# Expert weights in 2 MB stretches: one transfer fills two neighbouring places of the weight ring

## The chip, the cores and the metric

The kernel runs on one core of one Trainium2 chip, as one program with one launch. The metric is the device time in microseconds (us); lower is better. Before the change it is 2817.83 us, the median of three runs (2816.88 to 2820.12).

TensorE (PE in the profile) multiplies, VectorE (DVE) and ScalarE (ACT) do the elementwise work, SyncE (SP) issues nearly all transfers, and 16 DMA engines move the data.

## The reference

One sequence of 256 tokens of width 1024 goes through three transformer blocks in fp32: a block with three attention branches and a mixture of experts, a block with neighbourhood attention and pooling, and a block with a short convolution. The change touches only the mixture of experts:

```
logits = xt @ router_w + router_b;  top_v, top_e = top_k(logits, 4);  gate = softmax(top_v)
for each of 32 experts e, with the rows of the tokens that chose e:
    hb = xb @ w1[e] + b1[e]            # w1[e]: 1024 x 2048
    g, u = hb[:, :1024], hb[:, 1024:]
    g = min(g, 7);  u = clip(u, -7, 7)
    y = ((u + 1) * g * sigmoid(1.702 * g)) @ w2[e] + b2[e]    # w2[e]: 1024 x 1024
out[token] += gate * y
```

The weights of one expert are 12 MB in fp32, those of all 32 experts 384 MB. They are read from HBM once (and 12 MB more for the over turn named below).

## The kernel before

**The ring.** All weights pass through `ring`, a tile of 128 partitions with places of 8 KB each. In the expert stage eight places are in use. A slot is one use of a place: 1 MB, that is two chunks of 128 rows by 1024 columns. Slot j of the stage lies in place j % 8.

**A turn.** The stage is a loop of 16 turns, each for two experts, and after it an "over turn" of 12 slots for the busiest expert's tokens beyond 64. A turn uses 24 slots in this order: 0 to 3 gate columns of expert 0, 4 to 7 its up columns, 8 to 11 gate of expert 1, 12 to 15 up of expert 1, 16 to 19 down of expert 0, 20 to 23 down of expert 1 (`MOE_SLOTS`).

**What a slot goes through.** SP waits until the slot eight before has been used, then issues the transfer (`load_pair`, L692), which adds 16 to the semaphore of the place when it has landed. ACT waits for that semaphore and for the slot four before to have been used, and rounds the weights to `w_high` (`high`, L929; `w_high` has four places). DVE subtracts, in place over the ring, and leaves the rest as `w_low` (`low`, L2353). PE multiplies with `w_high` and then with `w_low` (`rows_gemm`, L1635, 4 + 4 matmuls per slot). The last matmul of a slot releases its place: it adds to `slots_used`, or, for every fourth slot, to `psum_full`. This is `MOE_RELEASE`, and SP waits for it.

**The order on the engines** is written out by hand. ACT: slots 4, 5, 6; copy of the gate rows (L964); slots 7, 8, 9, 10; copy of the up rows (L964); a small copy (L969); slot 11; the swish (L975); slots 12, 13, 14; L964; slots 15, 16, 17; rounding of the hidden layer of expert 0 (L982); slot 18; and so on to slot 3 of the next turn. DVE: slots 4 to 10; the gate half of expert 0 (L2380, L2386); slots 11 to 15; the up half of expert 0 (L2380, L2390, L2393); slot 16; the low part of the hidden layer (L2396); slots 17, 18; and later, near the turn's end, the sum of the results (L2405). PE cannot begin slot 16, the first of the down product, before L2396 has ended.

**The layout in HBM.** `slots(w)` lays a slot's 1 MB out in one stretch, with 8 KB for each partition, so that the slots of one half of one expert follow one another.

The functions that the change touches:

Of the kernel before, what the change touches and what calls it, by code (L numbers as in the profile page):

```python
# [16 lines left out]
P = 128  # L17
D = 1024
T = 256
DC = D // P  # L20
# [3 lines left out]
N_EXPERTS, TOP_K = 32, 4  # L24
# [20 lines left out]
SLOT = 2 * D  # L45
# [3 lines left out]
RING2, HIGHS = 8, 4  # L49
# [87 lines left out]
class Plan:  # L137
# [15 lines left out]
    def placed(self):  # L153

        while len(self.place) < len(self.stream):
            s = len(self.place)
            self.next = (self.next + 1) % self.places if s else 0
            self.place.append(self.next)
            self.before.append(self.holder.get(self.next))
            self.times[self.next] = self.times.get(self.next, 0) + 1  # L160
            self.landing.append(self.times[self.next])
            self.holder[self.next] = s

# [186 lines left out]
PLAN = make_plan()  # L350
# [56 lines left out]
def build(nc, ins, out):  # L407
    with ExitStack() as ctx:
        def sb(name, shape, dt=F32):
            return ctx.enter_context(nc.sbuf_tensor(name, shape, dt))  # L410
# [3 lines left out]
        def sem(name):  # L414
            if name not in sems:
                sems[name] = ctx.enter_context(nc.semaphore(name))
            return sems[name]
# [7 lines left out]
        ring = sb("ring", [P, RING, SLOT])  # L425
# [62 lines left out]
        at = 4096  # L488
# [56 lines left out]
        landed = [sem(f"slot_landed{i}") for i in range(RING)]  # L545
# [25 lines left out]
        def await_slot(pe, s):  # L571

            pe.wait_ge(landed[PLAN.place[s]], 16 * PLAN.landing[s])
# [6 lines left out]
        def slot_ap(s, rows=2, cols=D):  # L580
            return ring[:, PLAN.place[s], 0:rows * cols].rearrange("p (k n) -> p k n", k=rows)
# [33 lines left out]
        class Turn:  # L615
# [40 lines left out]

            def await_slot(self, eng, j):

                place = PLAN.place[PLAN.moe_slot + j]
                times = j // RING2 + 1 if self.x else PLAN.landing[PLAN.moe_slot + j]  # L660
                eng.wait_ge((landed_x if self.x else landed)[place],
                            self.turn * (16 * TURN_SLOTS // RING2) + 16 * times)
# [18 lines left out]

        def load_pair(sp, c, before_turn=None, slots=range(TURN_SLOTS)):

            for j, at in enumerate(slots):
                name, e, k, half = MOE_SLOTS[at]
                if j < RING2 and before_turn:
                    before_turn(j)
                else:
                    c.await_used(sp, j - RING2)
                src = ins[name][c.experts[e]][half * (DC // 2) + k // 2].rearrange("p (k n) -> p k n", k=2)  # L690
                place = PLAN.place[PLAN.moe_slot + j]
                sp.dma_start(slot_ap(PLAN.moe_slot + j), src).then_inc((landed_x if c.x else landed)[place], 16)  # L692

        def rounds_loop(eng, before_pairs, body):

# [9 lines left out]
        landed_x = [sem(f"slot_landed_x{i}") for i in range(RING2)]  # L705
# [13 lines left out]
        def _(sp):  # L719
# [15 lines left out]
            def before_first(j):  # L735
                if PLAN.before[PLAN.moe_slot + j] is not None:
                    await_release(sp, PLAN.before[PLAN.moe_slot + j])

            load_pair(sp, first_turn(0), before_first)
            with sp.Fori(1, PAIRS) as i:  # L740
                load_pair(sp, first_turn(i))
            load_pair(sp, over_turn(busiest_expert(sp)), None, OVER_AT)
            with sp.If(many(sp) > CAP):

# [23 lines left out]
        def _(act):  # L768
# [104 lines left out]
            def high_piece(n):  # L873

                s = PLAN.slots[f"mpiece{n}"]
                if n < 2:
                    await_release(act, PLAN.piece_before[n])
                else:
                    await_unit(act, U[f"mpiece{n - 2}"])
                await_slot(act, s)  # L880
                act.activation(piece_parts(n)[0], slot_ap(s, DC, 2 * P), ACT.Copy).then_inc(sem("piece_high_ready"), 1)
# [179 lines left out]
            def high_parts(until):  # L1061

                while highs[0] < len(PLAN.split_at) and PLAN.split_at[highs[0]] < until:
                    m = highs[0]
                    s = PLAN.split_at[m]
                    cols = PLAN.stream[s][5]
                    if m < HIGHS:
                        await_release(act, moe_end - HIGHS + m)
                    else:
                        await_release(act, PLAN.split_at[m - HIGHS])  # L1070
                    await_slot(act, s)
                    act.activation(high_ap(m, cols), slot_ap(s, 2, cols), ACT.Copy).then_inc(sem("w_high_ready"), 1)  # L1072
                    highs[0] += 1
# [128 lines left out]
        def _(pe):  # L1202
            def gemm(name, k_chunks, n_chunks, operands, parts_ready=None, halves_last=False):
# [17 lines left out]
                def await_parts(k):  # L1221
                    if k % 2 == 0:
                        if parts_ready:
                            parts_ready(k)
                        await_slot(pe, slots[k // 2])
# [1532 lines left out]
```

## Time and profile before

| | |
|---|---|
| device time, median of 3 runs | 2817.83 us (2816.88 to 2820.12) |
| span of the profiled execution | 2811.8 us |
| own time of the profiled execution | not listed apart; the median of the runs is 6.0 us above its span |
| PE busy | 2709.9 us, 96% |
| DVE busy | 2100.9 us, 75% |
| ACT busy | 1575.8 us, 56% |
| mean granted TensorE clock | 0.975 |
| expert transfers | 396 of 1024 KB |
| one turn of the expert stage (from issue to issue of slot 4) | 64.73 us |

The expert stage lies between about 440 and 1500 us of the span, slices 7 to 21 of the 40 in which the page cuts the span. Busy shares over the whole span hide that this stage has limits of its own: here DVE and the DMA engines are busy nearly all the time as well, so the stage has to be read by itself. In a row, "A <- B" after a time means that A sat idle until B released it. A row with x3 or x4 merges neighbouring instructions of one kind: its start is that of the first, its length that of all.

### The profile page before, as it was taken

What the parts mean: (1) busy time and instruction counts of PE and PEld (TensorE: products, weight loads), DVE (VectorE), ACT (ScalarE), POOL (GpSimd) and SP (SyncE); (2) the same over time, 40 slices, a digit from 0 to 9 for tenths busy, and PEclk for the clock granted to TensorE, in tenths of its full rate; (3) what the DMA queues carried; (4) which work ended last, traced back from release to release, by engine and by line L of the source; (5) the groups of instructions that cost most, each with busy time, mean ns of one, the idle gap of its engine ahead of it and who ended that gap; (6) DMA issues with size and microseconds to landing.
All of it is one profiled execution on the core that took longest, in us unless ns stands there. A gap on an engine that the chain in (4) does not pass through costs nothing.

```text
span 2811.8 us, 43791 instructions
## 1 busy us (share of the span) xinstructions
PE 2709.9 (96%) x17682; PEld 2472.9 (88%) x17682; DVE 2100.9 (75%) x1766; ACT 1575.8 (56%) x1410; POOL 0.4 (0%) x6
## 2 busy tenths in 40 slices
PE   6999999999999999999998999999989999999998
PEld 5889888888888888888886999999879999999998
DVE  6347649999999999999998787785545866754553
ACT  0045318888888888888884443353434434432442
POOL 0000000000000000000000000000000000000000
PEclk9999898999999999999998999999999999999999
DMA  9744448999999999999995876776317767754561
GB/s 391 255 164 135 151 171 329 381 380 388 389 385 392 390 390 393 394 390 382 386 379 199 297 251 255 258 266 243 142 65 251 283 222 262 270 178 165 165 194 62
DMA packets 172691, 776.11 MB, mean 276 GB/s; under 512 B 12272, under 2 KB 38000, under 8 KB 121616
## 3 DMA queue, kind: packets, MB, share of 16 engines
q1 hardware_dynamic: 168640, 768.71, 72.3%
q10 hardware_dynamic: 3920, 5.49, 0.7%
q8 instruction: 103, 1.69, 0.2%
q14 instruction: 28, 0.23, 0.0%
HBM read 773.10 MB, written 1.05 MB: 275 GB/s over the span
## 4 chain that ended last, share of the span: by engine, by line
PE 82%; DVE 11%; issue 3%; ACT 3%; DMA 0%; SPq 0%; DVEq 0%; ACTq 0%
PE psum L1257 38%; PE psum L1635 18%; PE psum L1211 7%; DVE w_low L2353 6%; PE psum L1675 4%; PE psum L1612 2%; PE psum L1653 2%; PE psum L1336 2%; ACT w_high L929 1%; PE psum L1355 1%; PE psum L1397 1%; PE psum L1492 1%; DVE arena L2380 1%; PE psum L1445 1%; PE psum L1520 1%
## 5 line engine op out<-in xcount | busy, mean ns | idle before, releaser
L2353 DVE TENSOR_TENSOR w_low<-ring,w_high 128x2048 fp32r<-128x2048 f32 x396 | 885.1, 2287 | 31.6 <-ACT w_high L929 20.5
L929 ACT ACTIVATE w_high<-ring 128x2048 fp32r<-128x2048 f32 x396 | 736.2, 1905 | 47.9 <-PE psum L1635 47.9
L1072 ACT ACTIVATE w_high<-ring 128x2048 fp32r<-128x2048 f32 (+1 forms) x199 | 362.4, 1829 | 561.2 <-PE psum L1257 478.0
L2489 DVE TENSOR_TENSOR w_low<-ring,w_high 128x2048 fp32r<-128x2048 f32 (+1 forms) x199 | 432.7, 2184 | 320.3 <-ACT w_high L1072 317.4
L1257 PE MATMUL psum<-h_high,w_high 128*128 128x256 f32 x2080 | 588.5, 283 | 21.6 <-ACT h_high L1085 20.4
L1257 PE MATMUL psum<-h_high,w_low 128*128 128x256 f32 x2080 | 590.6, 284 | 0.0
L1257 PE MATMUL psum<-h_low,w_high 128*128 128x256 f32 x2080 | 588.2, 284 | 0.0
L1257 PEld LDWEIGHTS psum<-h_high,w_high 128*128 128x128 f32 x2080 | 399.6, 192 | 24.1 <-issue 22.2
L1257 PEld LDWEIGHTS psum<-h_low,w_high 128*128 128x128 f32 x2080 | 394.9, 191 | 0.0
L1257 PEld LDWEIGHTS psum<-h_high,w_low 128*128 128x128 f32 x2080 | 394.5, 190 | 0.0
L1635 PE MATMUL psum<-w_high,xg 128*128 128x512 f32 x1056 | 296.0, 402 | 0.6 <-ACT xg L957 0.6
L1635 PE MATMUL psum<-w_low,xg 128*128 128x512 f32 x1056 | 291.7, 398 | 0.1
L1924 DVE SCALAR_TENSOR_TENSOR mod_sums<-ring,cs,mod_sums 128x1024 f32<-128x1024 f32 x203 | 257.4, 1282 | 12.7 <-DMA ring<-in_mod_w 8.5
L1257 PE MATMUL psum<-m_high,w_high 128*128 128x256 f32 x880 | 247.7, 281 | 0.8 <-DVE arena L2529 0.8
L1257 PE MATMUL psum<-m_low,w_high 128*128 128x256 f32 x880 | 247.2, 281 | 0.0
L1257 PE MATMUL psum<-m_high,w_low 128*128 128x256 f32 x880 | 247.2, 281 | 0.0
L1635 PEld LDWEIGHTS psum<-w_low,xg 128*128 128x128 f32 x1056 | 197.3, 188 | 54.6 <-DVE w_low L2353 7.0
L1635 PEld LDWEIGHTS psum<-w_high,xg 128*128 128x128 f32 x1056 | 196.7, 189 | 45.5 <-issue 0.8
L1635 PE MATMUL psum<-w_high,hid 128*128 128x512 f32 x528 | 153.8, 414 | 22.9 <-DVE hid L2396 22.9
L1257 PEld LDWEIGHTS psum<-m_high,w_high 128*128 128x128 f32 x880 | 165.8, 188 | 1.0 <-DVE arena L2529 0.9
L1257 PEld LDWEIGHTS psum<-m_low,w_high 128*128 128x128 f32 x880 | 165.8, 188 | 0.1
L1257 PEld LDWEIGHTS psum<-m_high,w_low 128*128 128x128 f32 x880 | 165.8, 188 | 0.0
(288 smaller groups left out, 3441.5 us busy)
## 6 DMA issues: line engine op xcount, KB each, us to landing
ring<-in_exp_w SPq DMA_DIRECT2D x396, 1024.0 KB, 8.7
ring<-in_ffn_w SPq DMA_DIRECT2D x135, 1024.0 KB, 5.3
ring<-in_mod_w SPq DMA_DIRECT2D x96, 1024.0 KB, 5.6
ring<-in_ffn_w SPq DMA_DIRECT2D x40, 768.0 KB, 4.7
ring<-in_w_in SPq DMA_DIRECT2D x24, 1024.0 KB, 8.9
ring<-in_even_w_in SPq DMA_DIRECT2D x12, 1024.0 KB, 7.2
ring<-in_conv_w_in SPq DMA_DIRECT2D x12, 1024.0 KB, 5.1
ring<-in_w_branch SPq DMA_DIRECT2D x6, 1024.0 KB, 5.5
```

The lines of the kernel that those rows point to most:

```text
L929: act.activation(high_ap(j, D), slot_ap(PLAN.moe_slot + j), ACT.Copy).then_inc(sem("expert_high_ready" + c.x), 1)
L1072: act.activation(high_ap(m, cols), slot_ap(s, 2, cols), ACT.Copy).then_inc(sem("w_high_ready"), 1)
L1211: mm = pe.matmul(unit(u0 + j // 4)[:, (j % 4) * T:(j % 4 + 1) * T], w[:, k % 2, (c0 + j) * P:(c0 + j + 1) * P], rhs(k), start=(k == 0 and ...
L1257: return pe.matmul(unit(u0 + j // 4)[:, (j % 4) * T:(j % 4 + 1) * T], w[:, k % 2, j * P:(j + 1) * P], h[:, k, :], start=first, stop=stop, ...
L1336: mm = pe.matmul(unit(u)[:, at:at + 1], mod_sums[:, MOD_BUFFERS[n][c], j * P:(j + 1) * P], ones[:, 0:1], start=True, stop=True)
L1612: mm = pe.matmul(cols[:, n, :, part * CAP:(part + 1) * CAP], h_nat[:, b, k * P:(k + 1) * P], sel[:, b, :, :], start=(b == 0), stop=(b == T ...
L1635: mm = pe.matmul(u[:, cols], x_parts(k), w[:, k % 2, cols], start=(k == 0 and w is wh), stop=(k == DC - 1 and w is wl), skip_group_check=True)
L1653: mm = pe.matmul(u[:, k * CAP:(k + 1) * CAP], moe_buf(rows)[:, k * P:(k + 1) * P], const("fold"), start=True, stop=True)
L1675: mm = pe.matmul(c.unit(name)[:, (k % 4) * T:(k % 4 + 1) * T], moe_buf(f"y_rows{e}")[:, k * P:(k + 1) * P], moe_buf(f"selT{e}"), start=(e ...
L1924: last = dve.scalar_tensor_tensor(part, w[:, k % 2, :], cond, part, ALU.mult, ALU.add)
L2353: dve.tensor_tensor(low_ap(PLAN.moe_slot + j, D), slot_ap(PLAN.moe_slot + j), high_ap(j, D).bitcast(F32), ALU.subtract).then_inc(sem("expe ...
L2489: dve.tensor_tensor(low_ap(s, cols), slot_ap(s, 2, cols), high_ap(m, cols).bitcast(F32), ALU.subtract).then_inc(sem("w_split"), 1)
```

## The change

The layout keeps four chunks (two slots) together, so that a partition's 16 KB for slots j and j+1, with j even, lie in one piece. `load_pair` goes through the slots in steps of two: it waits for the release of the odd slot's place, and issues one transfer of 2 MB into places j % 8 and j % 8 + 1. Only the even place's semaphore is incremented, and whoever waits for an odd slot waits for the semaphore of the even one. The bookkeeping of how often a place has been filled (`placed`) leaves the odd places of this stage out. The layouts of the other stages, their transfers, and the order of work on ACT, DVE and PE stay.

```
@@ placed @@
-            self.times[self.next] = self.times.get(self.next, 0) + 1
+            with_other = self.stream[s] is None and self.next % 2
+            self.times[self.next] = self.times.get(self.next, 0) + (0 if with_other else 1)
@@ await_slot @@
+                j -= j % 2
                 place = PLAN.place[PLAN.moe_slot + j]
@@ load_pair @@
-            for j, at in enumerate(slots):
+            for j, at in list(enumerate(slots))[::2]:
                 name, e, k, half = MOE_SLOTS[at]
                 if j < RING2 and before_turn:
                     before_turn(j)
+                    before_turn(j + 1)
                 else:
-                    c.await_used(sp, j - RING2)
-                src = ins[name][c.experts[e]][half * (DC // 2) + k // 2].rearrange("p (k n) -> p k n", k=2)
+                    c.await_used(sp, j + 1 - RING2)
+                src = ins[name][c.experts[e]][half * (DC // 4) + k // 4]
                 place = PLAN.place[PLAN.moe_slot + j]
-                sp.dma_start(slot_ap(PLAN.moe_slot + j), src).then_inc((landed_x if c.x else landed)[place], 16)
+                two = ring[:, place:place + 2, :].rearrange("p s n -> p (s n)")
+                sp.dma_start(two, src).then_inc((landed_x if c.x else landed)[place], 16)
@@ slots @@
-        pairs = w.reshape(N_EXPERTS, DC // 2, 2, P, -1, D)
-        return pairs.transpose(0, 4, 1, 3, 2, 5).reshape(N_EXPERTS, -1, P, SLOT)
+        fours = w.reshape(N_EXPERTS, DC // 4, 4, P, -1, D)
+        return fours.transpose(0, 4, 1, 3, 2, 5).reshape(N_EXPERTS, -1, P, 2 * SLOT)
```

SP's order at the start of the loop over turns, slots 0 to 3 of a turn, before:

```order
L692 ISA [waits slots_used]
L692 DMA ring<-in_exp_w 128x2048
L655 REGISTER_ALU
L692 ISA [waits slots_used]
L692 DMA ring<-in_exp_w 128x2048
L655 REGISTER_ALU
L692 ISA [waits slots_used]
L692 DMA ring<-in_exp_w 128x2048
L653 ISA
L692 ISA [waits psum_full]
L692 DMA ring<-in_exp_w 128x2048
```

The same place after the change:

```order
L696 ISA [waits slots_used]
L696 DMA ring<-in_exp_w 128x4096
L654 ISA
L696 ISA [waits psum_full]
L696 DMA ring<-in_exp_w 128x4096
```

Two transfers of twice the width stand where four stood, and each waits for what the odd slot's transfer waited for.

ACT's order from slot 8 to slot 12 of a turn, before (`slot_landed0` is the semaphore of place 0; L964 and L969 copy out of PSUM, L975 is the swish):

```order
L929 ACTIVATE w_high<-ring 128x2048 [waits slot_landed0]
L655 REGISTER_ALU
L929 ACTIVATE w_high<-ring 128x2048 [waits slot_landed1,slots_used]
L655 REGISTER_ALU
L929 ACTIVATE w_high<-ring 128x2048 [waits slot_landed2,slots_used]
L638 REGISTER_ALU
L964 ACTIVATE arena<-psum 128x1024 [waits psum_full]
L638 REGISTER_ALU
L969 ACTIVATE arena<-psum 128x256 [waits psum_full]
L661 REGISTER_ALU [waits psum_full]
L929 ACTIVATE w_high<-ring 128x2048 [waits slot_landed3]
```

and after:

```order
L933 ACTIVATE w_high<-ring 128x2048 [waits slot_landed0]
L656 REGISTER_ALU
L933 ACTIVATE w_high<-ring 128x2048 [waits slot_landed0,slots_used]
L656 REGISTER_ALU
L933 ACTIVATE w_high<-ring 128x2048 [waits slot_landed2,slots_used]
L639 REGISTER_ALU
L968 ACTIVATE arena<-psum 128x1024 [waits psum_full]
L639 REGISTER_ALU
L973 ACTIVATE arena<-psum 128x256 [waits psum_full]
L933 ACTIVATE w_high<-ring 128x2048 [waits slot_landed2,psum_full]
```

The order of the work is the same; slots 8 and 9 now wait for one semaphore, and so do slots 10 and 11. A register instruction has gone ahead of slot 11 (one more stands ahead of slot 12 instead, outside these rows).

## Rows read from the trace of the kernel before

**Rows 1.** The page: busy time, then DMA share and GB/s in 40 slices.

```profile
PE 2709.9 (96%) x17682; PEld 2472.9 (88%) x17682; DVE 2100.9 (75%) x1766; ACT 1575.8 (56%) x1410; POOL 0.4 (0%) x6
...
DMA  9744448999999999999995876776317767754561
GB/s 391 255 164 135 151 171 329 381 380 388 389 385 392 390 390 393 394 390 382 386 379 199 297 251 255 258 266 243 142 65 251 283 222 262 270 178 165 165 194 62
```

**Rows 2.** Busy time in one turn: us; PE, PEld, DVE, ACT, POOL; clock, DMA, GB/s.

```profile
942.90:1007.63 64.73, 63.27 (x326) 53.08 (x325) 62.79 (x41) 56.95 (x45) 0.00 (x0) 1.00 0.96 388
```

**Rows 3.** Waits, 500 to 1480 us: total us, times, longest.

```profile
ACT w_high L929 <- PE psum L1635: 45.0, 35, 2.4
...
PE psum L1635 <- DVE hid L2396: 22.0, 15, 1.5
DVE w_low L2353 <- ACT w_high L929: 16.2, 30, 1.5
```

**Rows 4.** Waits of SP's queue, 500 to 1480 us.

```profile
SPq L692 <- PE psum L1635: 769.1, 363, 6.6
```

**Rows 5.** Chain of waits, 960 to 992 us: start, length, what.

```profile
971.37 2.29 DVE w_low L2353
973.66 0.61 DVE arena L2380
...
974.83 0.02 ACTq L661
974.85 0.06 issue
974.91 0.04 ACTq L655
...
975.29 1.91 ACT w_high L929
...
983.84 2.29 DVE w_low L2353
...
990.12 0.61 DVE hid L2396
990.73 0.12 issue
990.85 1.20 PE psum L1635 x4
```

**Rows 6.** Timeline of SP: issues of slots 4, 5, 8, 9, 10, 11.

```profile
942.90 0.33 SPq L692 DMA_DIRECT2D ring<-in_exp_w  x1
944.77 0.33 SPq L692 DMA_DIRECT2D ring<-in_exp_w  x1
...
955.61 0.33 SPq L692 DMA_DIRECT2D ring<-in_exp_w  x1
957.47 0.33 SPq L692 DMA_DIRECT2D ring<-in_exp_w  x1
959.33 0.33 SPq L692 DMA_DIRECT2D ring<-in_exp_w  x1
961.20 0.33 SPq L692 DMA_DIRECT2D ring<-in_exp_w  x1
```

**Rows 7.** The tile ring: issue to landing of slots 4, 8, 9, 10, 11, in order.

```profile
DMA to landing us min/median/max: 4.7/4.7/4.7
...
DMA to landing us min/median/max: 4.8/4.8/4.8
...
DMA to landing us min/median/max: 6.1/6.1/6.1
...
DMA to landing us min/median/max: 7.2/7.2/7.2
...
DMA to landing us min/median/max: 7.8/7.8/7.8
```

**Rows 8.** DMA with a full queue, 8 KB rows (970 to 990 us).

```profile
DMA packets 1165, 8.49 MB, mean 424 GB/s; under 512 B 129, under 2 KB 129, under 8 KB 129
```

**Rows 9.** DMA with a full queue, 4 KB rows (1738 to 1742 us, FFN weights).

```profile
DMA packets 440, 1.68 MB, mean 419 GB/s; under 512 B 31, under 2 KB 31, under 8 KB 440
```

**Rows 10.** Timeline of ACT: slots 4 to 6, 7 to 10, 12 to 14, 15 to 17.

```profile
955.56 5.57 ACT L929 ACTIVATE w_high<-ring 128x2048 fp32r<-128x2048 f32 x3 [1.11 <-PE psum L1635]
...
961.99 7.31 ACT L929 ACTIVATE w_high<-ring 128x2048 fp32r<-128x2048 f32 x4
...
975.29 5.51 ACT L929 ACTIVATE w_high<-ring 128x2048 fp32r<-128x2048 f32 x3
...
981.60 5.52 ACT L929 ACTIVATE w_high<-ring 128x2048 fp32r<-128x2048 f32 x3
```

**Rows 11.** DVE's slots by form, in the expert stage and in the later blocks.

```profile
L2353 DVE TENSOR_TENSOR w_low<-ring,w_high 128x2048 fp32r<-128x2048 f32 x362 | 809.1, 2287 | 27.1 <-ACT w_high L929 16.2 <-DVE arena L2405 7.1
...
L2489 DVE TENSOR_TENSOR w_low<-ring,w_high 128x2048 fp32r<-128x2048 f32 x137 | 312.0, 2291 | 197.3 <-ACT w_high L1072 195.3 <-DVE mod_sums L1924 0.8
```

## The prediction, made before the changed kernel was run

> **What bounds the kernel now.** I read the page first. PE is busy 96% of the span, and in slices 7 to 20, the expert stage, the DMA engines read 9 in every slice at 380 to 394 GB/s, where later stages read 5 to 7 [rows 1]. That looks like a stage bound by its transfers, which larger transfers could help. So the second view is the list of waits of the stage. It holds no wait of ACT, DVE or PE for a landing at all: ACT waits for PE, PE for DVE, DVE for ACT [rows 3]. SP in turn waited 769.1 us of these 980 us for PE to release places [rows 4]. So the transfers go as fast as PE frees places, and no engine is held up by one. The third view is one turn by itself: 64.73 us, of which PE is busy 63.27, DVE 62.79, ACT 56.95, and the DMA share is 0.96 [rows 2]. Four resources are within 12% of one another, so what counts is their order. The chain of waits, the fourth view, gives it: in the first half of the turn it runs along DVE (slot 10 at 971.37, the gate half, slots 12 to 15 with slot 15 at 983.84, the low part of the hidden layer at 990.12) and enters PE at 990.85 [rows 5]. PE sits idle just before that, 22.0 us in 15 turns, 1.47 each [rows 3]. Whatever holds DVE up between slot 10 and slot 16 therefore lengthens the turn one for one. What holds PE up there costs nothing until the 1.47 us are used.
>
> The question is then by how much the landings lead their users, since the change makes each even slot land with its odd neighbour. The lead is smallest after the two places in a turn where SP waits longest (up to 6.6 us [rows 4]) and the queue runs dry: ahead of slot 4 and ahead of slot 8. I follow slot 8.
>
> **What the change does to the landings.** Before, in the turn of rows 2: slot 8 is issued at 955.61 and lands 4.8 later, at 960.4; slot 9 at 957.47, landing at 963.6; slot 10 at 959.33, landing at 966.5; slot 11 at 961.20, landing at 969.0 [rows 6, 7]. With a full queue the rate is 424 GB/s [rows 8], so 1 MB (1.049e6 bytes) takes 2.47 us, a pair 4.95. The landings of slots 8 to 11 lie 3.2, 2.9 and 2.5 apart. So after a dry queue two transfers lose 0.7 and 0.4 us against the full rate, 1.1 to 1.2 together, and the fourth, issued 5.6 us after the restart, loses nothing.
>
> After, the pair 8/9 is issued when slot 9 was, 957.47. A first transfer of 1 MB on a dry queue needs 4.8; the second MB adds 2.47: it lands at 964.7. Pair 10/11 is issued at 961.20, while the first still runs, and lands 4.95 + x later, at 969.7 + x. Here x is what the second transfer after a dry queue loses. Its bounds are 0 (as in the full queue) and 1.2 (all that three transfers lost before). I take 0.45, the row of the third transfer, since it was issued 3.72 after the first one, and the second pair is issued 3.73 after its first. Pairs 12/13 and 14/15 follow at 4.95 each: 974.6 + x and 979.6 + x.
>
> **What ACT and DVE do with that.** ACT runs slots 7 to 10 from 961.99 in steps of 1.80 (7.31 for four, 1.9 for one [rows 10]), so slot 8 starts at 963.8 and slot 10 at 967.4. Slot 8 is now 0.9 late and slot 9 with it. Slot 10 waits for 969.7 + x, which is 2.3 + x late, and ends at 971.6 + x. DVE started slot 10 at 971.37 [rows 5]: the cover was 2.1 us, and it is used up. DVE is late by 0.25 + x. After slot 10 ACT still has L964, L969 and slot 11 before DVE's own gate half is done; with the rows' spacing of 3.0 us, slot 11 is rounded by 974.6 + x, when DVE wants it. The swish and slots 12 and 13 only follow DVE. Slot 14 would start at 978.9 (two steps after 975.29), now at 979.15 + x, but lands at 979.6 + x. It pushes L964 and slot 15, which came 2.7 after slot 14 (981.60 [rows 10]), to 982.3 + x, ending at 984.2 + x. DVE took slot 15 at 983.84 [rows 5]: it is now late by 0.4 + x in all, not in addition. From slot 16 on ACT has more lead on DVE than the lateness (slot 18 about 0.6, slot 20 about 0.2, and each then has over 2 us to DVE), so nothing more comes on top.
>
> Per turn: 0.4 + 0.45 = 0.85 us. Lower end: x = 0, and rows of 16 KB move a little faster; from 4 KB to 8 KB rows the rate went from 419 to 424 GB/s [rows 8, 9], 1.2%, so up to 0.06 a pair, 0.2 over four pairs: 0.2 per turn. Upper end: 0.4 + 1.2 = 1.6 per turn. I give the wider rows nothing in the sum.
>
> **The rest of the edits.** Slots 4 to 7: the pair 4/5 starts on a dry queue too. Issued at 944.77, where slot 4 was issued at 942.90 and took 4.7 [rows 6, 7], it lands at 944.77 + 4.7 + 2.47 = 951.9, and pair 6/7 at 956.9 + x. ACT takes slots 4 to 6 from 955.56 in steps of 1.8, so slot 6 at 959.2 [rows 10]: leads of 3.6 and 1.8, covered. Slots 16 to 23 and 0 to 3 are moved at most 2.5 + 0.7 + x, and the DMA queue again runs dry ahead of slot 4, so lateness is not handed from turn to turn. SP has half as many issues (12 a turn); it only ever waits, so nothing comes of it. The extra register instruction ahead of slot 12 on ACT stands on the chain: one such step with its issue took about 0.1 [rows 5]. It falls in the 0.15 by which slot 14's landing is the later of the two limits, so it adds nothing unless x is small. Layout in HBM and semaphore bookkeeping cost no time. Everything outside the stage keeps its transfers.
>
> **The sum.** 15 turns x 0.85 = 12.8; the first turn's slot 10 has about 0.1 more lead, 0.75; the over turn has slots 8 to 11 but no 12 to 15, so 0.25 + 0.45 = 0.7. Together 14.2 us on a span of 2811.8. The median of the runs lies 6.0 above the span, and nothing of the change touches that: 2817.8 + 14.2 = 2832. Lower end 16.5 x 0.2 = 3, upper end 16.5 x 1.6 = 26: 2821 to 2844.
>
> **A rule and the trace.** Before the change the landings with a full queue come at 2.47 us per MB, all data, so a transfer's fixed part costs nothing there; on a dry queue it shows as 4.8 - 2.47 = 2.3 us, and a turn has two dry starts before and after. The Trainium skill, "DMA: Bandwidth & Descriptors", section "Anatomy of one DMA", gives a fixed cost of about 2 us for each transfer besides bytes over 436 GB/s, and "SBUF — State Buffer" advises the largest single transfer where the transfers bind. Taken per transfer in sequence, that rule would save 12 x 2 = 24 us a turn, which the landings 2.5 us apart speak against. Taken per dry start it agrees with the 2.3 of the trace, and by it the first pair would land at 957.47 + 2 + 4.8 = 964.3 instead of 964.7.
>
> **The rivals.** (a) The cover holds: the pair lands about 0.3 us sooner than I add up (a first transfer of 2 MB may hide its slow start better, x = 0, faster wide rows), so slot 10 comes within 0.1 of DVE's time. Then 0.0 to 0.3 per turn, up to 5 us: 2818 to 2823, say 2820. For it: the cover of 2.1 against a lateness of 2.3 is a near thing. Against it: x was not 0 at either of the two places in rows 7.
> (b) The restart costs its full 1.2 us with two transfers as it did with three, or more, because each is twice as long: 1.6 and up per turn, 2844 and more. PE's 1.47 us of idle don't help, as they come from the same wait. For it: the loss may go with bytes after a dry start, not with the time from issue. Against it: the fourth transfer, 5.6 us on, lost nothing.
> (c) Faster. The mechanism: DVE and ACT read and write the ring while the DMA engines fill it, and fewer, wider rows disturb them less; the place is DVE's 24 slots a turn at 2287 ns. It decides if DVE's slot gets shorter by more than the 0.2 to 0.85 us a turn that the landings cost. But DVE takes 2287 in this stage at a DMA share of 0.96 and 2291 in the later blocks at 5 to 7 tenths [rows 11, 1]: there is nothing to give back. A gain of 0.5%, 11 ns a slot, 0.27 a turn would be 4 us: 2814 with no lateness at all.
> (d) The change doesn't do what it says: the rows of 16 KB are cut in two for the DMA engines. Then only the wide rows' 0.2 goes, and the sum above stands, as it doesn't use them.
>
> **How the numbers follow.** The forecast with (d), 0.35 to 1.4 us a turn or 2824 to 2840: 62%. (a): 20%. (b): 13%. (c): 5%. A measurement of this kernel tells about 0.2%, 5.6 us, from no change; the borders are 2812.2 and 2823.5. (a) lies within, (b) and the forecast above, and of (c) half would be within: slower 0.75, same 0.22, faster 0.03. The predicted time is that of the forecast, 2832. The range leaves out the far parts of (b) and of (c): 2818 to 2845.
>
> **What would show it.** In the profile after: 198 expert transfers of 2048 KB; a new wait "ACT w_high <- DMA ring" in every turn, some 2.5 us at slot 10 and under 1 us at slots 8 and 14; DVE's wait for ACT up from 16.2 us by 10 to 15; PE's wait for the hidden layer up from 1.47 to about 2.3 a turn; the turn at 65.6 instead of 64.73; DVE's slot unchanged at 2287 ns. If the ACT waits are there and the turn is not longer, the cover held, and (a) is right. If no ACT wait for a landing shows, the step on the pair's landing is wrong. If the turn is longer but PE's wait for the hidden layer is not, the loss lies in the second half of the turn, and my chain is wrong.

## The result

The changed kernel takes 2842.11 us (median of 4 runs, 2839.3 to 2843.05) against 2817.36 us, a ratio of 1.0093 with a 95% interval of 1.0076 to 1.0109. It is 0.9% slower, 24.7 us. A second series on another occasion gave 2840.4 against 2814.02, 1.0072 (1.0048 to 1.0097). The ratios and their intervals are the recorded ones, here and below. They are not the quotient of the two medians, and the two can lie 0.2% apart. The forecast was slower, at 2832, in a range of 2818 to 2845.

The page of the profile after: busy times, DMA share, and the costliest groups that answer to the expert stage.

```profile
PE 2722.8 (96%) x17682; PEld 2483.2 (87%) x17682; DVE 2105.5 (74%) x1766; ACT 1585.0 (56%) x1410; POOL 0.4 (0%) x6
...
DMA  9744448999999999999995776777417767754451
...
L2357 DVE TENSOR_TENSOR w_low<-ring,w_high 128x2048 fp32r<-128x2048 f32 x396 | 889.1, 2287 | 44.5 <-ACT w_high L933 32.9
L933 ACT ACTIVATE w_high<-ring 128x2048 fp32r<-128x2048 f32 x396 | 744.6, 1909 | 108.7 <-DMA ring<-in_exp_w 56.9
...
ring<-in_exp_w SPq DMA_DIRECT2D x198, 2048.0 KB, 9.9
```

The busy times moved by less than 1%, and DVE's slot takes the same 2287 ns as in [rows 11]. What is new is a releaser: ACT now waits for the DMA of `ring`. The list of waits, 500 to 1480 us, against [rows 3]:

```profile
ACT w_high L933 <- DMA ring<-in_exp_w: 50.2, 75, 1.5
...
DVE w_low L2357 <- ACT w_high L933: 27.6, 52, 1.5
PEld psum L1639 <- issue: 24.4, 14, 1.8
...
PE psum L1639 <- DVE hid L2400: 16.6, 11, 1.5
...
PE psum L1639 <- DVE w_low L2357: 11.4, 15, 0.9
...
PE psum L1639 <- ACT w_high L933: 6.0, 4, 1.5
```

There are 75 waits of ACT for a landing in 15 turns, five a turn. DVE's wait for ACT went from 16.2 to 27.6, and PE has a second stop, for DVE's `w_low`, of 0.76 a turn. The stop of 1.5 us ahead of slot 16 is still there in every turn: 11 times the view puts it down to DVE, and 4 times to ACT (6.0 us), 22.6 us together against 22.0 before.

Now the turns one by one, from DVE's slot 4 to its next: length, busy us of PE, PEld, DVE, ACT, POOL, then granted clock, DMA share, GB/s. The first row of each block is all 16 turns together, the others are single turns. Of before:

```profile
436.57:1476.47 1039.90, 1016.91 (x5195) 853.12 (x5194) 1004.75 (x641) 911.68 (x704) 0.00 (x0) 1.00 0.96 388
...
762.58:828.72 66.14, 64.67 (x326) 54.13 (x325) 62.95 (x41) 57.23 (x45) 0.00 (x0) 0.97 0.94 381
```

Of after:

```profile
434.62:1493.82 1059.20, 1022.54 (x5191) 856.11 (x5190) 1008.98 (x641) 920.98 (x704) 0.00 (x0) 0.99 0.93 380
...
899.41:966.58 67.17, 64.78 (x326) 54.17 (x325) 63.16 (x40) 57.67 (x45) 0.00 (x0) 0.97 0.92 375
966.58:1031.92 65.34, 63.23 (x326) 53.03 (x325) 62.96 (x40) 57.51 (x45) 0.00 (x0) 1.00 0.94 385
```

All 16 turns together took 1059.2 us instead of 1039.9, 19.3 more. Two things are in it. A turn at full clock takes 65.3 to 65.7 instead of 64.73 (the first and the last turn have other lengths in both kernels). And turns with a granted clock of 0.97 take 66.96 to 67.17 where a full one takes 65.3 to 65.7, some 1.6 more. Before had two of these among its 16 turns; after had five, and a sixth fall of the clock in its first turn.

Outside the stage the two spans differ by 8.4 us (27.7 less 19.3), though nothing there was changed but the over turn, for which the sum had 0.7 us. From the end of these windows to the end of the span it is 2811.8 - 1476.5 = 1335.3 before and 1345.7 after:

```profile
1476.47:2811.80 1335.33, 1291.97 (x10213) 1261.34 (x10211) 849.21 (x763) 533.31 (x448) 0.15 (x2) 0.98 0.61 212
...
1493.82:2839.50 1345.68, 1301.89 (x10213) 1270.86 (x10211) 849.64 (x763) 533.26 (x448) 0.15 (x2) 0.97 0.60 211
```

The same 10213 matmuls kept PE busy 9.9 us longer, at a lower granted clock. Added up from the trace, the clock stood at the lower of its two levels for 54 us of this stretch before and for 83 after. Less half of that time, the stretch is 1308 and 1304 us, and in all fourteen profiles between 1304 and 1310. In the twelve profiles of the experiments, none of which changes more of that part than its over turn, the stretch lies between 1336.3 and 1345.6, with 59 to 76 us at the lower level. So the profiled execution of before was the quickest of them all there, and that of after the slowest. About 19 of the 25 us lie in the expert stage. The rest goes with the clock behind it, where the profiles differ even between kernels that are alike there. Whether the changed stage has a part in it is not shown.

### The profile page after: what moved, and what is told of

Read it like the earlier page. It is cut to its first block and busy times, and to the rows that moved or that the text cites. A ratio compares the mean times of both kernels' runs of the same rounds, so it can differ in the third digit from the quotient of the medians.

```text
span 2839.5 us, 43045 instructions
## 1 busy us (share of the span) xinstructions
PE 2722.8 (96%) x17682; PEld 2483.2 (87%) x17682; DVE 2105.5 (74%) x1766; ACT 1585.0 (56%) x1410; POOL 0.4 (0%) x6
## 5 line engine op out<-in xcount | busy, mean ns | idle before, releaser
L2357 DVE TENSOR_TENSOR w_low<-ring,w_high 128x2048 fp32r<-128x2048 f32 x396 | 889.1, 2287 | 44.5 <-ACT w_high L933 32.9
L933 ACT ACTIVATE w_high<-ring 128x2048 fp32r<-128x2048 f32 x396 | 744.6, 1909 | 108.7 <-DMA ring<-in_exp_w 56.9
```

Of the source, the lines that this page charges most:

```text
L933: act.activation(high_ap(j, D), slot_ap(PLAN.moe_slot + j), ACT.Copy).then_inc(sem("expert_high_ready" + c.x), 1)
L2357: dve.tensor_tensor(low_ap(PLAN.moe_slot + j, D), slot_ap(PLAN.moe_slot + j), high_ap(j, D).bitcast(F32), ALU.subtract).then_inc(sem("expe ...
```

## The experiments

In all that follow, "a turn" is read as above, from DVE's slot 4 to the next, at full clock where nothing else is said. The times stand against runs of the kernel before on the same chip.

**1. The late issue alone.** SP waits as in the changed kernel, transfers stay as before:

```
                 if j < RING2 and before_turn:
-                    before_turn(j)
-                else:
-                    c.await_used(sp, j - RING2)
+                    if j % 2 == 0:
+                        before_turn(j)
+                        before_turn(j + 1)
+                elif j % 2 == 0:
+                    c.await_used(sp, j + 1 - RING2)
```

> The old layout and 1 MB transfers with a semaphore each, but SP waits for the odd slot's place before it issues both of a pair, one right behind the other. Theory A (the loss needs the late issue and the joint signal together: only then does slot 10 come later than the 2.1 us by which ScalarE leads VectorE there): slot 8 lands about 4.8 after the issue, 1.5 before ScalarE wants it, slot 10 at most 0.5 late, inside the cover; turn 64.7 to 64.9 us, time within 3 us of before. Rival B (the late issue alone is the loss, by an idle DMA queue): turn 65.4, time +20 us or more. Rival C (the layout in HBM or the wide rows are the loss): as before, turn 64.73.

2818.45 against 2816.27, ratio 0.9999 (0.9989 to 1.0009). The turn is 64.7:

```profile
958.61:1023.31 64.70, 63.23 (x326) 53.06 (x325) 62.74 (x40) 56.96 (x45) 0.00 (x0) 1.00 0.94 389
```

Waiting for the odd place costs nothing. Rival B falls. The issues and landings of slots 8 to 11 in this turn, each issue followed by its own landing:

```profile
957.94 0.33 SPq L694 DMA_DIRECT2D ring<-in_exp_w  x1
...
DMA to landing us min/median/max: 4.7/4.7/4.7
...
958.46 0.33 SPq L694 DMA_DIRECT2D ring<-in_exp_w  x1
...
DMA to landing us min/median/max: 6.8/6.8/6.8
...
961.66 0.33 SPq L694 DMA_DIRECT2D ring<-in_exp_w  x1
...
DMA to landing us min/median/max: 6.0/6.0/6.0
...
962.17 0.33 SPq L694 DMA_DIRECT2D ring<-in_exp_w  x1
...
DMA to landing us min/median/max: 8.0/8.0/8.0
```

Counted from the first issue they land at 4.7, 7.3, 9.7 and 12.2, some 2.5 apart: issued in twos, 0.52 apart, the transfers of 1 MB lose nothing after the dry start. In [rows 6] they were issued 1.9 apart and lost 1.1 to 1.2.

**2. The joint signal alone.** Whoever uses an even slot waits for both landings:

```
+                for q in (j, j + 1) if j % 2 == 0 else (j,):
+                    place = PLAN.place[PLAN.moe_slot + q]
                     ...
+                    eng.wait_ge((landed_x if self.x else landed)[place],
                     ...
```

> The old layout, 1 MB transfers issued as before, but whoever needs an even slot waits until the odd one has landed too. Theory A: slot 10 is rounded 1.6 to 1.7 us later, inside the 2.1 us of cover; turn 64.73 to 64.9, time within 3 us of before, and ScalarE shows waits for landings at slots 10 and 14. Rival B: as before. A rival D (the joint signal alone is the loss) would give a turn of 65.4 and +20 us.

2821.6 against 2816.27, 1.0012 (0.9996 to 1.0028); eleven turns at full clock take between 64.69 and 64.95 and one 65.21.

```profile
1159.75:1224.44 64.69, 63.23 (x326) 53.06 (x325) 62.75 (x40) 57.24 (x45) 0.00 (x0) 1.00 0.97 389
```

ACT's busy time went up by 0.3 us a turn here, the usual turn did not. Rival D, with its 20 us, falls too: the median is 5 us higher, and the interval ends at 0.28%, 8 us.

**3. The layout alone.** New layout, and transfers of 1 MB, 8 KB rows that lie 16 KB apart:

```
+                src = ins[name][c.experts[e]][half * (DC // 4) + k // 4][:, k // 2 % 2 * SLOT:(k // 2 % 2 + 1) * SLOT] \
                     ...
```

> The new layout, but transfers of 1 MB as before: rows of 8 KB, 16 KB apart in HBM. Theory A: nothing changes, turn 64.73, landings 2.48 us apart, time within 2 us of before. Rival C: the landings are further apart than 2.5 us and the turn is longer.

2814.97 against 2816.27, 0.9993 (0.9977 to 1.001), with turns of 64.71. Rival C falls as far as the layout goes: where the rows lie in HBM has no part in it. Rows of 16 KB come only with transfers of 2 MB, so this run does not test them.

**What 1 to 3 leave open.** Theory A says that the late issue and the joint signal together are the loss. No run has just these two, with transfers of 1 MB. Experiment 1 allows an estimate. There slots 9 and 11 land 6.61 and 11.58 us after DVE's slot 4, in the median of the turns. The pairs of the changed kernel, whose first issue comes at the same time (0.67 before slot 4 in both), land at 7.05 and 11.94. So the joined transfer itself comes 0.4 later than two single ones issued one right behind the other. With the joint signal on the landings of experiment 1, slot 8 would be 0.9 to 1.1 late for ACT, inside DVE's cover of 1.27, and DVE would be 0.3 to 0.5 late at slot 10, where the changed kernel has 0.79. By this estimate the late issue and the joint signal explain about half of DVE's lateness, and the later landing of the joined transfer the other half.

**4 and 5. Which pairs.** The changed kernel with pairs for some slots and single transfers for the others (`JOINT` lists the pairs; single odd slots have their own semaphore again):

```
+                both = j - j % 2 in JOINT
+                if both and j % 2:
+                    continue
                 ...
+                    c.await_used(sp, j + both - RING2)
```

Once with all pairs but 8/9 and 10/11:

> As after, but slots 8 to 11 of each turn come in four transfers of 1 MB, each with its own issue and signal; the other twenty slots in ten pairs. Theory A: the loss is that of slots 8 to 11, and slots 12 to 15 have just enough lead: turn 64.7 to 64.9, time within 4 us of before. Rival E (every pair costs a little): turn about 65.3, +16 us or more.

2818.86 against 2816.27, 1.001 (0.9996 to 1.0024). Six turns take 64.7 and seven 64.9 to 65.3. The rest is at slot 15, where DVE is 0.23 late in the median turn. One more turn had a fall of the clock (67.7). The first turn took 67.5 instead of 65.6, which I did not follow up. Once with these two pairs only:

> As before, but slots 8/9 and 10/11 come as pairs of 2 MB with one signal, the other twenty slots in single transfers. Theory A: nearly the whole loss of after: turn 65.3 (0.6 at slot 10; slots 12 to 15 land one by one again), 12 to 20 us over before. Rival E (every pair costs a little): 2 to 4 us over before.

2834.1 against 2814.02, 1.0054 (1.0033 to 1.0075), 20 us. Turns of 65.3 to 65.6, and four more with a clock of 0.97. Of 12 pairs in a turn, two carry most of the loss: 20 us where the changed kernel, in the same series, has 26 (experiment 8), and nearly all of the longer turn.

**6 and 7. Each of the two by itself**, one run each.

> As before, but slots 8/9 come as one pair; slots 10 and 11 and all others single. Theory A: the pair lands at 7.7 after its issue and slot 10, 2.45 to 2.5 later, about 1.0 past ScalarE's time, within the 2.1 us of cover: turns without a fall of the clock 64.73. A rival H (any late landing there costs its own lateness): about 65.0 to 65.3.

2818.72 against 2816.38, with turns of 64.8 to 65.0 and no fall of the clock. DVE's seven slots 4 to 10, first in the kernel before:

```profile
958.15 15.51 DVE L2353 TENSOR_TENSOR w_low<-ring,w_high 128x2048 fp32r<-128x2048 f32 x7 [0.41 <-DVE arena L2405]
```

and with this pair:

```profile
890.36 15.67 DVE L2373 TENSOR_TENSOR w_low<-ring,w_high 128x2048 fp32r<-128x2048 f32 x7 [0.41 <-DVE arena L2425]
```

That is 0.16 longer. The lateness is not at slot 10, which is covered as expected, but at slot 8: ACT's lead there was 1.26 to 1.27, and slot 8 was 1.3 to 1.4 late. I had not worked out that cover. The turns lie between theory A's 64.73 and rival H's 65.0 to 65.3.

> As before, but slots 10/11 come as one pair, all others single. Theory A: the pair lands about when slot 11 did, 1.6 past ScalarE's time for slot 10 or a little more, within the cover: 64.73. Rival H: 65.0 or more.

2826.09 against 2816.38, 9.7 us in a single run. Nine of the 16 turns are as before, and two more within 0.2 us. Two are at 65.4, two of those with a low clock read 67.2 and 67.8 instead of 66.1, and the last 66.8 instead of 65.2. The cover is just used up: after ACT's slot 10 DVE starts its own 0.1 later in the median turn, where it had 2.08. Without the falls of the clock (none with pair 8/9, four with pair 10/11, two before), the 16 turns are longer by 0.15 and 0.35 us each on the mean, and by 0.8 with both pairs (experiment 5). Rival H, that a late landing costs its whole lateness, does not hold: slot 8 came 1.3 to 1.4 late and cost 0.16.

**8. The changed kernel again.**

> The changed kernel once more, beside the kernel before on the same chip. Theory A with the clock: turns without a fall of the granted clock about 65.3 to 65.6 us, five to seven turns with one at about 67, time 18 to 26 us over before. If the extra 8 us in the stages after the experts belonged to the change, they would be there again; if they are the run's own clock, the time outside the expert stage is within 5 us of the other profiles.

2840.4 against 2814.02, 26 us. The 16 turns took 1060.7 us, with six falls of the clock; the rest of the span 2841.4 - 1497.9 = 1343.5. Stage and falls are those of the first profile.

**9. VectorE late without any change to the transfers.** One instruction more in the kernel before, whose result nobody uses:

```
                 low(c, 4, 5, 6, 7, 8, 9, 10)
+                dve.tensor_reduce(small[:, 461:462], vecs[:, 0:560], AX_X, ALU.max)
                 gate_half(0)
```

> The kernel before, its transfers untouched, with one more VectorE instruction of about 0.6 us a turn (a maximum over 560 columns, its result unused) between slot 10 and the gate half of expert 0. Theory A: a lateness of VectorE there lengthens the turn one for one, 64.73 to about 65.35, as in after; and if TensorE's longer idle time is what makes the granted clock fall in more turns, five to seven turns instead of two or three read about 66.9: 16 to 20 us over before. Rival F (the falls come with the transfers or by chance): 10 us over before and two or three such turns. Rival G (the loss in after is not VectorE's slot 10): no longer turn, the instruction is hidden.

2830.53 against 2814.02, 1.0053 (1.0036 to 1.0069), 16.5 us. Two turns of its profile:

```profile
828.42:895.32 66.90, 64.79 (x326) 54.23 (x325) 63.57 (x42) 57.21 (x45) 0.00 (x0) 0.97 0.93 376
895.32:960.68 65.36, 63.26 (x326) 53.07 (x325) 63.39 (x42) 56.93 (x45) 0.00 (x0) 1.00 0.95 385
```

The turn is 0.63 longer, for an instruction of 0.73 that delays DVE's next one by 0.65. And there are four turns at a clock of 0.97, where five to seven were expected and before had two. PE's stops, 500 to 1480 us, are nearly those of after, and no engine waits for a landing:

```profile
PE psum L1635 <- DVE hid L2396: 21.9, 15, 1.5
PE psum L1635 <- DVE w_low L2353: 9.7, 15, 0.7
```

This is nearly the picture of the changed kernel, made with DVE alone. Rival G falls. Of rival F the transfers fall as the cause of the longer turn; chance does not yet, since experiments 1 to 3 have three falls each without a longer turn, and four is only one more.

**10. Twice that**, over 1120 columns (1.32 us).

> As the kernel with the late VectorE, but the unused maximum is over 1120 columns, about 1.3 us. Theory A: turns of 64.73 + 1.3 less the 0.08 that the first left hidden, about 65.95, still one for one, and as many or more turns with a lower clock at 1.55 us each: 24 to 34 us over before. Rival: TensorE's longer idle time makes the clock fall in nearly every turn: 40 us and more.

2843.94 against 2816.38, 1.01 (1.0083 to 1.0117), 27.6 us. Turns of 65.93, and nine at 67.4 to 67.9:

```profile
968.42:1035.89 67.47, 64.78 (x326) 54.23 (x325) 64.17 (x41) 57.22 (x45) 0.00 (x0) 0.97 0.93 373
1035.89:1101.82 65.93, 63.25 (x326) 53.08 (x325) 64.00 (x42) 56.97 (x45) 0.00 (x0) 1.00 0.94 383
```

Again nearly one for one (1.20 for an instruction of 1.32, whose start overlaps its neighbour's end), and 1.54 for each fall of the clock, within theory A's 24 to 34 us. Nine falls speak against chance. With PE's idle time of 1.5, 2.1 and 2.7 us a turn, 2, 4 and 9 of the 16 turns had a lower clock.

**11. A shorter chain, in the kernel before.** DVE does the up half of expert 0 ahead of slot 15, PE turns the gate rows of expert 1 ahead of slot 15, and DVE's slot 16 comes behind the hidden layer:

```
-                low(c, 11, 12, 13, 14, 15)
-                up_half(0, 16)
-                low(c, 17, 18)
+                low(c, 11, 12, 13, 14)
+                up_half(0, 15)
+                low(c, 16, 17, 18)
@@ PE
-                project("up1", 1, 12)
-                turn_rows("gate1_turn", "gate1", "gate_rows", 1)
+                project("up1", 1, 12, lambda: turn_rows("gate1_turn", "gate1", "gate_rows", 1))
```

The function given to `project` runs ahead of its last slot, 15. The edits of `project` and of the order of the PSUM units are left out here.

> The kernel before with the chain that the experiments point to made shorter: VectorE does the up half of expert 0 ahead of slot 15 instead of behind it, and slot 16 behind the hidden layer's low part; TensorE turns the gate rows of expert 1 ahead of slot 15. Theory A (VectorE from slot 10 to the hidden layer bounds half the turn, and TensorE has 1.47 us idle there): about 1 us less a turn, 63.7, and fewer turns with a lower clock: 12 to 20 us under before. If the second half of the turn or the transfers bound it as closely: less than 5 us.

2811.59 against 2814.02, 0.9983 (0.9969 to 0.9998): 2.4 us faster than the kernel before. The expected 1 us a turn, 12 to 20 us in all, is not there:

```profile
886.94:951.48 64.54, 63.71 (x326) 52.98 (x325) 62.75 (x41) 56.82 (x45) 0.00 (x0) 1.00 0.97 390
```

The turn is 0.19 shorter. DVE is at slot 18 at the same time after its slot 4 as before, 34.89: the order changed, its sum of work did not, and it has no gap to give. But PE's 1.45 us in one piece is gone (its longest stop is 0.7), and in this profile the clock did not fall once in 16 turns: 1033.9 us for the stage. Over whole runs this does not show: the granted clock is 0.974 in the median of the 12 runs, and 0.975 in the 22 of before.

**12. The changed kernel with that chain.**

> The changed kernel with the shorter chain of the kernel with the up half sooner. Theory A: slot 10 is as late as in after, so the turn is 64.53 + 0.6, about 65.15; if the falls of the clock hang on the 1.5 us of idle ahead of the hidden layer, which is gone here, there are none or few in the stage: 6 to 12 us over before. If they hang on the whole idle time of a turn, two to six remain and it is 10 to 20 us over before.

2835.66 against 2816.38, 1.0066 (1.0044 to 1.0087). That is 19 us over before, where 6 to 12 were expected. The turn is 65.5 to 65.9, not 65.15, and the clock did not fall in the 16 turns; all four runs have a granted clock of 0.975 to 0.977, those of the changed kernel in the first series 0.969 to 0.971. One of its turns on DVE:

```profile
834.37 13.50 DVE L2361 TENSOR_TENSOR w_low<-ring,w_high 128x2048 fp32r<-128x2048 f32 x6 [0.41 <-DVE arena L2413]
848.33 2.29 DVE L2361 TENSOR_TENSOR w_low<-ring,w_high 128x2048 fp32r<-128x2048 f32 x1 [0.46 <-ACT w_high L933]
...
865.27 0.69 DVE L2404 TENSOR_TENSOR hid<-arena,hid 128x512 fp32r<-128x512 f32 x1 [0.39 <-ACT hid L986]
```

Beside the 0.7 up to slot 10 there are 0.39 ahead of the hidden layer's low part. ACT's rounding of it (L986) stands behind slots 16 and 17 in ACT's order, and these waited for their pair to land. In the shorter chain this wait is no longer covered. PE stood idle for 30.4 us between 500 and 1480 us, twice a turn, never longer than 1.2 us at once, and kept its clock; the kernel of experiment 9 had 31.6 us with a stop of 1.5 in each turn and lost it four times.

## Why the prediction was right, and where it fell short

**The limits of the stage: right.** The chain along DVE from slot 10 to the hidden layer sets the first half of the turn; experiments 9 and 10 lengthen it one for one. That holds for making it longer alone. Experiment 11 took the 1.5 us stop away and won 0.19 a turn and not 1, because the sum of DVE's work in the turn stayed.

**The landings: right in sum, each part a little off.** Issues of SP for the pairs 8/9, 10/11, 12/13 and 14/15, in the turn that begins at 966.58 on DVE, after the change:

```profile
965.91 0.33 SPq L696 DMA_DIRECT2D ring<-in_exp_w  x1
...
969.63 0.33 SPq L696 DMA_DIRECT2D ring<-in_exp_w  x1
...
973.36 0.33 SPq L696 DMA_DIRECT2D ring<-in_exp_w  x1
...
977.10 0.33 SPq L696 DMA_DIRECT2D ring<-in_exp_w  x1
```

and their times from issue to landing, in the same order:

```profile
DMA to landing us min/median/max: 7.6/7.6/7.6
...
DMA to landing us min/median/max: 8.7/8.7/8.7
...
DMA to landing us min/median/max: 9.9/9.9/9.9
...
DMA to landing us min/median/max: 11.1/11.1/11.1
```

Counted from the first issue the pairs land at 7.6, 12.4, 17.4 and 22.3. I had 7.2, 12.7, 17.6 and 22.6. The first was 0.3 to 0.4 later than 4.8 + 2.47, which two single transfers issued in twos do keep (7.3 in experiment 1). The loss x ahead of the second, taken at 0.45, was 0; the later ones came 4.9 apart. At slots 10 and 14 the errors cancel to 0.3.

**DVE's lateness: right in size.** Predicted 0.70 at slot 10 and 0.85 in all. The timeline of DVE in the same turn of after, and its gap at slot 10:

```profile
966.58 13.38 DVE L2357 TENSOR_TENSOR w_low<-ring,w_high 128x2048 fp32r<-128x2048 f32 x6 [0.41 <-DVE arena L2409]
980.39 2.29 DVE L2357 TENSOR_TENSOR w_low<-ring,w_high 128x2048 fp32r<-128x2048 f32 x1 [0.43 <-ACT w_high L933]
...
986.25 8.93 DVE L2357 TENSOR_TENSOR w_low<-ring,w_high 128x2048 fp32r<-128x2048 f32 x4 [0.30 <-ACT w_high L933]
```

From slot 4 to slot 10 it takes 13.81 here, where before it took 13.22 (971.37 of [rows 5] less 958.15, the row in experiment 6), 0.59 more; in the median turn 0.79, of which 0.23 arise at slot 8. I had not counted these: I compared slot 8 with ACT's time and not with DVE's. ACT's 0.9 of lateness, as predicted, would have stayed inside DVE's cover of 1.27; the pair landed 0.4 later, and ACT was 1.3 late. Slots 12 to 15 add 0.03 here and 0.04 in the median, not 0.15. The median turn is 0.83 late at slot 15. The 16 turns grew by 19.3 - 4 x 1.55 = 13.1 us apart from the clock, against 13.6 in the sum (14.2 with the over turn).

**What hides the rest: right.** All pairs but 8/9 and 10/11 together cost 0.2 us a turn at full clock on the mean, and the whole kernel is at most 0.24% slower by the interval (experiment 4); what there is of it lies at slot 15. The layout and the later issue cost nothing (1 and 3). Wide rows on their own were not tested; the rate with them was 428 GB/s against 424.

**The step that failed: the sum had no term for the clock.** "What holds PE up there costs nothing until the 1.47 us are used", I wrote, and took the idle time as a free cover. Before, that same stop already went with two falls of the granted clock to half (2.4 to 1.2 GHz) for 3.4 us in 16 turns, at 1.5 us each; after, with a second stop of 0.6 to 0.9 us in the turn, there were six in both profiles of the changed kernel. That is 4 x 1.55 = 6 us of the 25, and together with the 13 it is the 19 of the stage. Where the falls stand in the turn is in the trace. PE's first matmuls of slot 16 in one turn of after, and the clock us by us:

```profile
933.01 1.40 PE L1639 MATMUL psum<-w_high,hid 128*128 128x512 f32 x4 [1.50 <-DVE hid L2400]
...
933.00:934.00 1.00, 0.99 (x4) 0.86 (x5) 1.00 (x1) 1.00 (x3) 0.00 (x0) 0.92 0.89 377
934.00:935.00 1.00, 1.00 (x3) 0.78 (x3) 1.00 (x1) 1.00 (x1) 0.00 (x0) 0.50 1.04 442
```

All 45 falls in the turns of the fourteen profiles begin like this one, between 0.3 us before and 1.0 us after the end of a stop of 1.5 us; none begins at the second stop. Experiments 9 and 10 show that more falls come with a later DVE when no transfer is touched. Experiments 11 and 12 had none, without the stop of 1.5 us; that is one profile each, and one kernel with the stop had none either (experiment 6). The remaining 5 to 6 us lie outside the stage, with the clock there, as read above, and the sum has no term for them either. The prediction's rows ([rows 2 to 5]) come from the profile that was quickest outside the stage, and runs of the kernel before ranged from 2805.7 to 2828.2. The 6.0 us that I added from the span to the median were of two kinds: each run's time is 1.7 to 1.8 above its own span, and the profiled run of before was the quickest of its four, 2813.46.

**How much of the hit is luck.** The forecast proper was 2824 to 2840 us, and the measured 2842 lies just above it. It is inside the stated range because that was widened for rival (b), whose mechanism did not happen. The way and the cause of the longer turn were forecast; of the 24.7 us the sum holds 14.2.

**The signs.** 198 transfers, ACT's wait for landings in every turn, DVE's unchanged slot and DVE's wait up by 11.4 came as said. ACT's wait was 1.2 at slots 8 and 10 and 0.2 at slot 14, where I had said under 1 at slot 8 and some 2.5 at slot 10: slot 8's lateness had already pushed slots 9 and 10. PE's wait for the hidden layer did not grow from 1.5 to 2.3; PE waited the difference earlier, for slot 11's `w_low`, since it follows DVE there as well:

```profile
986.01 1.19 PE L1639 MATMUL psum<-w_low,xg 128*128 128x512 f32 x4 [0.60 <-DVE w_low L2357]
...
999.91 1.19 PE L1639 MATMUL psum<-w_high,hid 128*128 128x512 f32 x4 [1.50 <-DVE hid L2400]
```

By my own sign, a longer turn without a longer wait for the hidden layer, the loss would lie in the second half of the turn. It does not: DVE is 0.83 late at slot 15 already. The sign was badly chosen.

**The rivals.** (a), that the cover holds, was the nearer thing than its 20% said for a single pair, as experiments 6 and 7 show, but not for both. (b) did not happen: after the dry start the first large transfer lost 0.3 to 0.4 and the second nothing, where three small ones lost 1.1 to 1.2. The loss of the small ones went with their spacing, not with bytes after the dry start: issued in twos they lost nothing (experiment 1). (c) has nothing for it. (d) is excluded: between 985 and 1000 us, with a full queue, the changed kernel moved 6.42 MB in 440 packets, 48 of them under 512 B, so the others hold 16 KB each. The rate was 428 GB/s, 1% over [rows 8], and it did not matter.

**Fixed cost per transfer.** The Trainium skill, "DMA: Bandwidth & Descriptors", section "Anatomy of one DMA — SWDGE (gpsimd) path", gives for one DMA about 2.0 us plus bytes over 436 GB/s. The section is about transfers issued from GpSimd, and these are issued from SyncE. An estimate by it for 2 MB is 6.8 us; the pair on a dry queue took 7.6 from issue to landing. Behind a full queue the pairs came 4.9 apart, where the bytes over the page's 436 GB/s alone would take 4.8. So halving the number of transfers saved nothing that the stage could use.

## What to carry to other kernels

A joined transfer is issued only when its last place is free, and it gives its first half to its user only when the second has landed. Here it also landed 0.4 us later than two single ones issued one right behind the other. Before joining transfers, read for each of them how long its landing leads its user, and that user's lead over the engine that sets the end. Only where the queue has run dry just before is the answer close, and a few single transfers there keep the rest free to be joined. Where the chain runs along one engine, an idle time of TensorE is no free cover: it may cost clock.

## What the runs showed of the hardware

- **The granted clock and one stop of 1.5 us.** In 16 turns with PE's longest stop at 1.5 us it fell 2, 4, 6 and 9 times as the idle time of the stage (500 to 1480 us) went from 22.1 to 31.6 (experiment 9), 34.0 (after, twice) and 40.3 us (experiment 10). Experiments 4 and 5 fit in, with one fall at 23.8 us and four at 32.9. Each fall began at the end of a stop of 1.5 us. In two kernels with 12.6 and 30.4 us of idle time and no stop over 1.2 us it did not fall. The kernels of experiments 1 to 3, with 22.0 to 22.6 us of idle time, had three falls each, and those of experiments 6 and 7 (one run each, 24.6 and 27.2 us) none and four, so chance has a part, and what exactly decides stays open. Each fall lasted 3.4 us and cost 1.4 to 1.7 us in most turns.
- **A dry queue and the spacing of issues.** Three transfers of 1 MB issued 1.9 us apart after a dry start lost 1.1 to 1.2 us against the full rate. Issued in twos, 0.52 apart, they lost nothing (landings at 4.8, 7.3, 9.8 and 12.3 in the median turn of experiment 1). One transfer of 2 MB landed at 7.7 in the median turn, 0.4 behind the two single ones, and the pair behind it lost nothing more.
- **DVE beside a busy DMA.** A 128x2048 subtraction took 2287 ns with rows of 8 KB and of 16 KB landing in the same tile.
